# Gate rows of the mLSTM spread from a high and a low part, and the bound's exponential moved

## The reference

```python
log_f = log_sigmoid(f_pre)              # [head, t]
F = cumsum(log_f)                       # g_F in the kernel
u = i_pre - F                           # g_u
M = max(0, cummax(u))                   # g_M;   m_t = F + M   (g_G)
w[t, s] = exp(u[s] - M[t]) for s <= t   # weights of head h
num = (q k^T * w) @ v;  den = sum_s (q k^T * w)
h = num / max(|den|, exp(-m_t))
```

## Time and profile before

| | us |
|---|---|
| median of 3 runs | 1425.88 (1425.37 to 1426.09) |
| the profiled execution, its own time | 1428.8 |
| its span, first to last instruction | 1426.1 |
| TensorE busy | 1401.7 |
| VectorE busy | 1147.6 |
| ScalarE busy | 822.8 |
| granted TensorE clock, mean | 0.996 |

### The profile page before, as it was taken

The page is one execution under the profiler, slowest core; times in us unless marked ns, Lnnn a source line. Parts: engine busy times, 40 slices in busy tenths (PEclk is TensorE's granted clock), DMA queues, the critical chain, the costliest instruction groups (busy, mean ns, idle before and its releaser), DMA issues.

```text
span 1426.1 us, 25528 instructions
## 1 busy us (share of the span) xinstructions
PE 1401.7 (98%) x10325; PEld 1312.9 (92%) x10325; DVE 1147.6 (80%) x1805; ACT 822.8 (58%) x1245; POOL 10.5 (1%) x21
## 2 busy tenths in 40 slices
PE   8999999999999999999999999999999999999997
PEld 8898888888888888889999999998999999999986
DVE  7898888888898888887778777777787887777763
ACT  6776776445776775344656555444446575644552
POOL 2000000000000000000000000000000000000000
PEclk9999999999999999999999999999999999999998
DMA  9544999986446999988754578898787556778661
GB/s 263 157 143 117 285 265 272 292 226 163 134 140 191 272 263 297 278 245 225 213 148 148 176 235 224 220 252 227 231 230 217 147 151 184 228 208 235 179 186 65
DMA packets 485363, 297.12 MB, mean 208 GB/s; under 512 B 14956, under 2 KB 455792, under 8 KB 485120
## 3 DMA queue, kind: packets, MB, share of 16 engines
q1 hardware_dynamic: 483728, 292.00, 72.9%
q10 hardware_dynamic: 816, 1.84, 0.4%
q0 software_dynamic: 704, 1.66, 0.3%
HBM read 289.43 MB, written 1.05 MB: 204 GB/s over the span
## 4 chain that ended last, share of the span: by engine, by line
PE 78%; DVE 13%; issue 3%; ACT 3%; DMA 2%; SPq 1%; DVEq 0%; ACTq 0%
PE acc L1938 15%; PE acc L1939 15%; PE acc L1940 14%; PE acc L1955 8%; PE mx L1955 6%; DVE w_lo L1082 5%; PE acc L1956 4%; PE mx L1956 3%; DVE ada_acc L1172 3%; ACT w_hi L583 1%; PE acc L1970 1%; PE acc L1972 1%; PE acc L1971 1%; DMA raw<-in_w_down 1%; DMA rotb<-projb 1%
## 5 line engine op out<-in xcount | busy, mean ns | idle before, releaser
L1082 DVE TENSOR_TENSOR w_lo<-raw,w_hi 128x1024 fp32r<-128x1024 f32 x450 | 541.6, 1221 | 111.2 <-ACT w_hi L583 109.4
L583 ACT ACTIVATE w_hi<-raw 128x1024 fp32r<-128x1024 f32 x450 | 458.0, 1049 | 135.5 <-DMA raw<-in_w_in 82.5
L1938 PE MATMUL acc<-h,w_hi 128*128 128x258 f32 (+1 forms) x1776 | 509.4, 287 | 7.6 <-DVE h L1109 2.8
L1939 PE MATMUL acc<-h,w_hi 128*128 128x258 f32 (+1 forms) x1776 | 503.8, 284 | 0.0
L1940 PE MATMUL acc<-h,w_lo 128*128 128x258 f32 (+1 forms) x1776 | 498.0, 280 | 0.0
L1938 PEld LDWEIGHTS acc<-h,w_hi 128*128 128x128 f32 x1776 | 334.4, 188 | 15.1 <-issue 4.7
L1940 PEld LDWEIGHTS acc<-h,w_lo 128*128 128x128 f32 x1776 | 338.5, 191 | 0.0
L1939 PEld LDWEIGHTS acc<-h,w_hi 128*128 128x128 f32 x1776 | 335.3, 189 | 2.6 <-issue 2.4
L1955 PE MATMUL mx<-u,w_hi 128*128 128x512 f32 x864 | 302.2, 392 | 0.0
L1956 PE MATMUL mx<-u,w_lo 128*128 128x256 f32 x864 | 243.6, 282 | 0.0
L1955 PEld LDWEIGHTS mx<-u,w_hi 128*128 128x128 f32 x864 | 162.2, 188 | 33.2
(11 more groups left out here) (294 smaller groups left out, 1642.8 us busy)
## 6 DMA issues: line engine op xcount, KB each, us to landing
raw<-in_w_in SPq DMA_DIRECT2D x132, 512.0 KB, 4.1
ada<-in_w_ada SPq DMA_DIRECT2D x96, 512.0 KB, 5.1
raw<-in_w_ffn_in SPq DMA_DIRECT2D x88, 512.0 KB, 4.6
raw<-in_w_up SPq DMA_DIRECT2D x64, 512.0 KB, 5.9
raw<-in_w_down SPq DMA_DIRECT2D x64, 512.0 KB, 6.5
raw<-in_w_out SPq DMA_DIRECT2D x32, 512.0 KB, 4.1
raw<-in_w_ffn_out SPq DMA_DIRECT2D x32, 512.0 KB, 4.2
raw<-in_w_ret_o SPq DMA_DIRECT2D x16, 512.0 KB, 4.1
```

Source lines behind the costliest of these rows:

```text
L583: nc.scalar.activation(w_hi[:, n % NS], raw[:, n % NS], ACT.Copy).then_inc(hi_ready, 1)
L1082: V.tensor_tensor(w_lo[:, n % NS], raw[:, n % NS], w_hi[:, n % NS].bitcast(F32), ALU.subtract).then_inc(lo_ready, 1)
L1938: mm(outp, w_hi[:, i % NS, k], rhs[:, k, 0], start=k == 0, stop=False)
L1939: mm(outp, w_hi[:, i % NS, k], rhs[:, k, 1], start=False, stop=False)
```

## The change

- `gate_rows` multiplied a [4, 128] selection with g_M in plain f32. Now VectorE splits g_M into a part rounded to f32r (rows 0 to 3 of `g_M2`, 36 rows) and the rest (rows 32 to 35), and TensorE runs one f32r matmul a head with a [36, 128] selection, a column of `pick` repeated. Two memsets a layer clear `g_M2` and `g_G2`; four copies in `rest_of_vectors` build `pick` and `pick_pairs`.
- The bound's argument F + M is added and clipped in its argument (`G_LOW`, `G_HIGH`), split likewise into `g_G2`, and spread; the exponential is taken by ScalarE on the spread [128, 512] in place of the copy to `ebc`, and stands in front of the silu. The exponential and the clip on [4, 256] go.
- TensorE's order: both `gate_rows` after slab 9 (they stood before it and after slab 10), `sums(0)` inside slab 10, `gate_columns` after slab 10. VectorE's: `lo_upto(13)` and `lo_upto(14)` behind `convolve(3)`.

```diff
@@ tiles and steps of ScalarE
+G_LOW, G_HIGH = -0.5 * math.log(1e30), -0.5 * math.log(1e-33)
...
+        pick = sb("pick", [36, 4], F32R)
+        pick_pairs = sb("pick_pairs", [36, 4, HD], F32R)
...
+                g_M2 = sb("g_M2", [36, S], F32R, until_values)
+                g_G2 = sb("g_G2", [36, S], F32R, until_values)
...
-                def forget_exp():
-                    act.wait_ge(f_G, l + 1)
-                    nc.scalar.activation(g_E[:], g_G[:], ACT.Exp, scale=-2.0).then_inc(f_E, 1)
...
                 def spread_exp():
                     act.wait_ge(f_uc, l + 1)
-                    nc.scalar.activation(ebc[:], mx[:, 0], ACT.Copy).then_inc(f_bcsb, 1)
+                    nc.scalar.activation(ebc[:], mx[:, 0], ACT.Exp, scale=-2.0).then_inc(f_bcsb, 1)
...
                 ahead(13)
-                forget_exp()
                 ahead(14)
                 head_square(0)
                 head_seed(0)
                 ahead(15)
+                spread_exp()
                 conv_silu()
                 spread_max()
-                spread_exp()
                 ahead(16)
@@ VectorE
             def rest_of_vectors():
                 dve.wait_ge(boot_t, 6)
+                boot.done(V.tensor_copy(pick[0:32], con[0:32, K_ID:K_ID + 4]))
+                boot.done(V.tensor_copy(pick[32:36], con[32:36, K_ID + 32:K_ID + 36]))
+                boot.done(V.tensor_copy(pick_pairs[0:32], con[0:32, K_ID:K_ID + 4].unsqueeze(2).to_broadcast([32, 4, HD])))
+                boot.done(V.tensor_copy(pick_pairs[32:36], con[32:36, K_ID + 32:K_ID + 36].unsqueeze(2).to_broadcast([4, 4, HD])))
...
-                    V.tensor_tensor(g_G[:], g_F[:], g_M[:], ALU.add).then_inc(f_G, 1)
-                    dve.wait_ge(f_G, l + 1)
-
-                def gates_clipped():
-                    dve.wait_ge(f_E, l + 1)
-                    V.tensor_scalar(g_E[:], g_E[:], 1e30, 1e-33, ALU.min, ALU.max).then_inc(f_E2, 1)
+
+                def gate_parts():
+
+                    c.link(V.tensor_copy(g_M2[0:4], g_M[:]))
+                    V.tensor_tensor(g_M2[32:36], g_M[:], g_M2[0:4].bitcast(F32), ALU.subtract).then_inc(f_parts, 1)
+
+                def bound_parts():
+
+                    c.link(V.tensor_tensor(g_G[:], g_F[:], g_M[:], ALU.add))
+                    c.link(V.tensor_scalar(g_G[:], g_G[:], G_HIGH, G_LOW, ALU.min, ALU.max))
+                    c.link(V.tensor_copy(g_G2[0:4], g_G[:]))
+                    V.tensor_tensor(g_G2[32:36], g_G[:], g_G2[0:4].bitcast(F32), ALU.subtract).then_inc(f_parts, 1)
...
                 c.done(V.memset(ones4[:], 1.0))
+                c.done(V.memset(g_M2[:].bitcast(F32), 0.0))
+                c.done(V.memset(g_G2[:].bitcast(F32), 0.0))
...
                 gate_maxima()
                 to_sbuf(7)
+                gate_parts()
                 convolve(2)
-                gates_clipped()
+                bound_parts()
                 to_sbuf(8)
+                lo_upto(p0 + 12)
+                convolve(3)
                 lo_upto(p0 + 14)
-                convolve(3)
                 gate_negated()
@@ TensorE
+                             (lambda k: norm_sum(l * 2) if k == (4 if l else 7) else None) if i == 1 else
+                             (lambda k: sums(0) if k == 3 else None) if i == 10 else None).then_inc(slab_used, 1)
...
                 def gate_rows(n):
-                    pe.wait_ge(s_con, 32)
-                    pe.wait_ge(f_M, l + 1)
+                    pe.wait_ge(f_parts, l * 2 + 1)
...
-                        ins = mm(mx[:, 1 + n, i * S:(i + 1) * S], con[0:4, K_SEL + h * P:K_SEL + (h + 1) * P], g_M[:],
+                        ins = mm(mx[:, 1 + n, i * S:(i + 1) * S], pick[:, h:h + 1].to_broadcast([36, P]), g_M2[:],
...
-                    pe.wait_ge(f_E2, l + 1)
+                    pe.wait_ge(f_parts, l * 2 + 2)
                     for n in range(2):
-                        ins = mm(mx[:, 0, n * S:(n + 1) * S], con[0:4, K_PAIR + n * P:K_PAIR + (n + 1) * P], g_E[:],
-                                 start=True, stop=True)
+                        ins = mm(mx[:, 0, n * S:(n + 1) * S], pick_pairs[:, 2 * n:2 * n + 2].rearrange("p h d -> p (h d)"),
+                                 g_G2[:], start=True, stop=True)
...
-                project(3, 4, 5, 6, 7, 8)
+                project(3, 4, 5, 6, 7, 8, 9)
                 gate_rows(0)
-                project(9)
-                sums(0)
+                gate_rows(1)
+                project(10)
                 gate_columns()
-                project(10)
-                gate_rows(1)
                 project(11, 12)
+                pe.wait_ge(f_bcsb, l * 3 + 2)
+                ml_scores(0)
                 pe.wait_ge(f_bcsb, l * 3 + 3)
-                ml_scores(0)
-                pe.wait_ge(f_bcsb, l * 3 + 2)
                 values(0)
```

More of the change, by code:

```diff
@@ L16 @@
+import math
 from contextlib import ExitStack
@@ L278, in program @@
             ones4 = sb("ones4", [4, S], F32, mix_a)
+            with ExitStack() as until_values:
+                g_M2 = sb("g_M2", [36, S], F32R, until_values)
+                g_G2 = sb("g_G2", [36, S], F32R, until_values)
             vtok = sb("vtok", [P, 3, 4, P], F32, mix_a)
@@ L372, in program @@
         cv_first = sem("cv_first"); cv_ready = sem("cv_ready"); cv_silu = sem("cv_silu")
-        f_abs = sem("f_abs"); f_ln = sem("f_ln"); f_M = sem("f_M"); f_G = sem("f_G"); f_E = sem("f_E"); f_E2 = sem("f_E2")
+        f_abs = sem("f_abs"); f_ln = sem("f_ln"); f_M = sem("f_M");
         f_bc = sem("f_bc"); f_bcsb = sem("f_bcsb"); f_uc = sem("f_uc"); f_ucsb = sem("f_ucsb")
-        f_exp = sem("f_exp"); ml_v = sem("ml_v"); ml_ln = sem("ml_ln"); ml_rs = sem("ml_rs")
+        f_parts = sem("f_parts"); f_exp = sem("f_exp"); ml_v = sem("ml_v"); ml_ln = sem("ml_ln"); ml_rs = sem("ml_rs")
         ml_s = sem("ml_s"); ml_arg = sem("ml_arg"); ml_w = sem("ml_w"); ml_p = sem("ml_p"); ml_nd = sem("ml_nd")
@@ L1325, in arguments @@
                         dve.wait_ge(s_con, 32)
-                    dve.wait_ge(f_bcsb, l * 3 + h // 2 + 1)
+                    dve.wait_ge(f_bcsb, l * 3 + h // 2 + 2)
                     if h >= 2:
@@ L1350, in ml_bounded @@
                     dve.wait_ge(ml_d, l + 1)
-                    dve.wait_ge(f_bcsb, l * 3 + 3)
+                    dve.wait_ge(f_bcsb, l * 3 + 1)
                     c.link(V.tensor_tensor(m_d, m_d, ebc[:], ALU.max))
```

1 line of the change is left out of this document (removed).

## The result

| | before | changed |
|---|---|---|
| median | 1425.99 (4 runs) | 1433.28 (1430.33 to 1435.74, 4 runs) |
| ratio | | 1.0051, 95% interval 1.0034 to 1.0069 |
| a second set of runs, five rounds | 1425.92 | 1431.27, ratio 1.0042 (1.0029 to 1.0055) |
| span of the profiled execution | 1426.1 | 1430.7 |

The change made the kernel slower by 0.4 to 0.5%, 5.3 to 7.3 us. The forecast was +1.65 us, in a range up to 1429.4.

A forecast was written before the change was run, and what follows sets the result against it. The prediction took TensorE as busy nearly throughout, with VectorE setting the end of the mixing part. Layer 0's +2.1 us and layer 1's -0.45 us gave +1.65 us, 1427.5 us on the median, range 1424.8 to 1429.4.

The forecast's parts named there:

- Everything behind runs relative to TensorE with at most eight slabs of prefetch, so both shifts reach the end.: Behind the mixing part: layer 0's +2.1 us and layer 1's -0.45 us carry through unchanged to the kernel's end.
- Layer 0 ends 2.1 us later: First block, layer 0: late `to_sbuf(8)` puts `sums(0)` 2.1 us late, and the lateness lasts to the layer's end.
- VectorE's sum: Layer 0, before `to_sbuf(8)`: memsets 0.26, picks 0.7, `gate_parts` 0.65, `bound_parts` 0.1 and 0.65, together 2.36 us.
- dear copies: Layer 0, VectorE: if copies don't run at double speed, its added steps sum to 2.6 us.
- the stand's length: Layer 0: TensorE waits some 1.6 us in slab 10 before `sums(0)`, in place of the wait removed.
- VectorE then has one idle stretch until `rope(4)`: Layer 0, late part: only the 0.92 us before `rot` is idle, on a transfer that is late too.
- The same two memsets stand at its start, 0.2 for the `w_lo`: Start of layer 1: the memsets delay the `w_lo` on which the next slabs hang, +0.2 us.
- Layer 1, -0.65 from there: Layer 1 after its memsets: `rope(4)` and the scores of pair 4 come 0.65 us early.
- VectorE had idle time there that ended on TensorE and on the rotation's transfer [...] so it can follow: Layer 1, around `ml_outputs(1)`: idle stretches of 0.3 and 0.7 us let VectorE follow TensorE, 0.7 us early.
- TensorE's saving: Rival, both layers: short row spreads save 2.4 us each plus a 0.3 wait, 5.1 us passing through; chance 0.12.
- The second rival: Row spreads, both layers: f32r spreads don't run in one pass, layer 1 about +2.5 us, total 1430.5; chance 0.08.
- The third rival: Layer 1 gives nothing back, as late `head_norm(0)` and the bound's exponential hold VectorE 0.5 to 1.0 late; 1428.9, chance 0.16.

The follow-up runs named there:

- tiles in place: Changed kernel with pick and pick_pairs declared at the end of the second block's space, so all other tiles lie as before: 1428.46 us, ratio 1.0020.
- the stand filled: Changed kernel plus 15 matmuls whose sums nobody reads, ahead of `sums(0)` in layer 0 only: 1430.04 us, ratio 1.0041.
- sums(0) late: Kernel before with only `sums(0)` moved from behind slab 9 to behind the third k of slab 10: 1429.21 us, ratio 1.0027.

## Why the prediction was wrong

**The size of the result.** The step that failed is "Everything behind runs relative to TensorE with at most eight slabs of prefetch, so both shifts reach the end." The shifts did reach the end, but the stretch behind was taken as unchanged, and it is not: the change declares two tiles ahead of `u2`, and the down matmuls slow down. 1.7 to 4 us of the 5.3 to 7.3 are that, a term that the forecast had at nothing. The diff had the two declarations, and the kernel has unused tiles named `before_h2`, `before_y2` and `before_u2` with no work of their own; I read over both.

With the tiles in place the changed kernel is at 1.0020 (1.0011 to 1.0028), +2.8 us (1.6 to 4.0), and my +1.65 lies just inside, at its lower edge. That near agreement is in part luck: in the same profile, counted from `norm_var`, pair 4 of layer 0 is 2.2 to 2.4 us late (2.1 was forecast), but layer 1 is 0.9 to 1.1 longer than in the kernel before and not 0.45 shorter. By its terms:

- "Layer 0 ends 2.1 us later": `sums(0)` was 2.49 late. VectorE's sum was mis-sized, 2.36 where 2.73 was measured, more than the 2.6 that I gave for dear copies: the picks 1.0 for 0.7, the two pairs of parts 0.75 and 0.87 for 0.65 and 0.75, while the memsets, 0.26, moved `norm_var` by 0.11 at most. The 0.27 us of slack at `sums(0)` held.
- Missing: the half clock after the stand, 0.96 us. I had the stand's length right (1.6 for 1.71) and priced it as nothing but its own time. It is not there in every execution: with its tiles in place the changed kernel has the same stand at full clock, and goes from `sums(0)` to pair 4 in 68.98 us, as with the stand filled (68.81).
- "VectorE then has one idle stretch until `rope(4)`": in the changed kernel it also waited 0.89 for the transfer of `rope(3)`. In layer 0 these waits sum to 1.15, 0 and 0.18 us in the three profiles of the changed kernel, against 0.92, 0.59 and 0.39 in the three of the kernel before, so they differ by execution, and this is a spread of about 1 us that the range should have held, not a cost of the change.
- "The same two memsets stand at its start, 0.2 for the `w_lo`": 0.38 (the layer's memset is 3.82 late, the `w_lo` 4.20).
- Layer 1, -0.65 from there: with no rotation's wait, in the kernel with the stand filled, 96.70 against 97.19, that is -0.49 with the memsets in it; in the changed kernel's two profiles +0.86 and +0.42, with waits of 1.71 and 1.44. With the tiles in place, waits of 0.35 and 1.41, it is +0.92. So the step that failed in layer 1 is "VectorE had idle time there that ended on TensorE and on the rotation's transfer [...] so it can follow": the early stretch came out as forecast (0.7 early at `ml_outputs(1)`), but the waits for the transfers behind it, 0.65 to 0.87 us in the kernel before, were 1.4 to 1.8 us in all three profiles of the changed kernel and took the gain back. Why they grew stays open.

**The cause named for layer 0** held for this kernel, 2.2 of 2.49 us, but was half the truth. I wrote that `weights(0)` follows `sums(0)`; the chain that makes this so is 18.7 us long and only 0.7 shorter than TensorE's own way, and so TensorE's saving is worth at most 0.7 us in layer 0 unless `sums(0)` also moves forward, and then the column spreads and ScalarE's list come next. That, with the tiles, is why taking VectorE's steps away did not make the change pay, and the chain is why "sums(0) late" costs 3.9 us with no new work at all.

**The rivals.** TensorE's saving did not pass through, though it is real: a pair fell from 1.02 to 0.33 us. The second rival's spreads at the old price were not seen (0.33, near two slab matmuls). The third rival, layer 1 giving nothing back, is what the three profiles of the changed kernel show, though by transfers and not by `head_norm(0)`. None had the tiles or the clock.

## What to carry to other kernels

When a change declares a tile, look at what lies behind it in SBUF: run the old kernel with an unused tile of that size in its place, which separates the move from the work in one run. A stand of TensorE of 1.7 us costs more than 1.7 us if the clock falls behind it (here by 0.96); filling it with matmuls shows the difference. And before shortening an engine's work, measure how much longer its way is than the chain beside it, here 0.7 us: only that much can be gained until the chain's first step is moved too, and behind that waits the next one.
